# First layer norm of a two-block layer: affine vectors applied at the transposed evacuation, the residual's later by token

## What is computed

```python
def layernorm(x, g, b):
    mu = jnp.mean(xf, axis=-1, keepdims=True)
    xc = xf - mu
    var = jnp.mean(xc * xc, axis=-1, keepdims=True)
    y = xc * lax.rsqrt(var + LN_EPS) * g + b

h = layernorm(x, ln_in_g, ln_in_b)
proj = h @ w_in[l]                       # 2048 x 7184
...
mix = jnp.concatenate([y_conv, y_m], axis=-1) @ w_out[l]
h = layernorm(ALPHA * h + mix, ln1_g[l], ln1_b[l])
```

## Time and profile before

| | us |
|---|---|
| median of three runs | 3107.63 (3106.39 to 3108.59) |
| the profiled execution | 3097.76 |
| its span | 3096.0 |
| TensorE matmul busy | 2666.7 (86%) |
| VectorE busy | 1770.5 (57%) |
| ScalarE busy | 881.6 (28%) |
| mean granted clock of TensorE | 0.985 |

### The profile page before, as it was taken

How to read it: one execution, slowest core, us unless ns; L and a number is a source line. 1 busy time by engine, 2 the same in 40 slices (tenths; PEclk the granted TensorE clock), 3 DMA queues, 4 the chain that set the end, 5 groups by cost and what they waited for, 6 DMA issues and landing times.

```text
span 3096.0 us, 33400 instructions
## 1 busy us (share of the span) xinstructions
PE 2666.7 (86%) x12561; PEld 1914.2 (62%) x12561; DVE 1770.5 (57%) x2212; ACT 881.6 (28%) x943; POOL 532.5 (17%) x532
## 2 busy tenths in 40 slices
PE   6999998677777777777777777999999999999998
PEld 6999888622222222222222237998877888888886
DVE  5456556855555555555555456544656656555445
ACT  3433433300011111111111004433444444444443
POOL 0000000344433343333334430000000000000000
PEclk9999999899999999999999998999999999999999
DMA  6554563899999999999999995544454555555553
GB/s 228 169 172 160 180 228 136 341 422 421 421 422 422 422 422 422 422 422 422 422 422 422 422 356 179 175 156 151 143 190 155 189 190 189 189 189 190 190 193 146
DMA packets 220040, 859.94 MB, mean 278 GB/s; under 512 B 17616, under 2 KB 20016, under 8 KB 147120
## 3 DMA queue, kind: packets, MB, share of 16 engines
q0 software_dynamic: 73728, 536.90, 41.9%
q1 hardware_dynamic: 146224, 321.79, 31.1%
HBM read 856.54 MB, written 2.10 MB: 277 GB/s over the span
## 4 chain that ended last, share of the span: by engine, by line
PE 60%; DMA 30%; DVE 5%; issue 3%; ACT 1%; POOL 0%; POOLq 0%; DVEq 0%; ACTq 0%
DMA vb<-in_peer_v,vidx 29%; PE PS L462 11%; PE PS L2002 7%; PE PS L1860 7%; PE PS L464 5%; PE PS L491 5%; PE PS L495 5%; PE PS L493 5%; PE PS L503 4%; PE PS L507 4%; PE PS L505 4%; DVE wl L396 1%; ACT wh L391 1%; DMA ub<-in_peer_v,vidx 1%; PE PS L1876 1%
## 5 line engine op out<-in xcount | busy, mean ns | idle before, releaser
L1860 PE MATMUL PS<-vb,diag 128*128 128x512 f32 x1920 | 890.0, 607 | 331.4 <-DMA vb<-in_peer_v,vidx 317.3
L396 DVE TENSOR_TENSOR wl<-raw,wh 128x2048 fp32r<-128x2048 f32 x292 | 669.3, 2292 | 732.0 <-ACT wh L391 730.4
L1860 PEld LDWEIGHTS PS<-vb,diag 128*128 128x128 f32 x1920 | 346.3, 190 | 874.4 <-issue 750.6
L1358 DVE CUSTOM_DVE_ANT_0 ub<-ub,RES 128x2048 f32<-128x2048 f32 x256 | 586.5, 2292 | 479.0 <-DMA ub<-in_peer_u,uidx 475.1
L391 ACT CAST wh<-raw 128x2048 fp32r<-128x2048 f32 x292 | 556.7, 1907 | 912.8 <-PE PS L495 292.7
L462 PE MATMUL PS<-XHL,wh 128*128 128x512 f32 x1408 | 488.2, 394 | 0.0
L491 PE MATMUL PS<-XHL,wh 128*128 128x256 f32 x1408 | 402.2, 286 | 7.8 <-DVE XHL L537 4.8
L495 PE MATMUL PS<-XHL,wl 128*128 128x256 f32 x1408 | 399.6, 284 | 0.0
L493 PE MATMUL PS<-XHL,wh 128*128 128x256 f32 x1408 | 399.6, 284 | 0.0
L464 PE MATMUL PS<-XHL,wl 128*128 128x256 f32 x1408 | 390.0, 277 | 0.0
L689 POOL DMA_INDIRECT ub<-in_peer_u,uidx x256 | 261.9, 1023 | 648.2 <-DVE uidx L1346 528.7
(11 more groups left out here) (304 smaller groups left out, 2166.6 us busy)
## 6 DMA issues: line engine op xcount, KB each, us to landing
raw<-in_w_in SPq DMA_DIRECT2D x112, 1024.0 KB, 5.1
raw<-in_w_ffn_gate SPq DMA_DIRECT2D x44, 1024.0 KB, 5.2
raw<-in_w_ffn_up SPq DMA_DIRECT2D x44, 1024.0 KB, 5.1
raw<-in_w_ffn_down SPq DMA_DIRECT2D x44, 1024.0 KB, 4.8
raw<-in_w_out SPq DMA_DIRECT2D x32, 1024.0 KB, 5.1
raw<-in_peer_wq SPq DMA_DIRECT2D x16, 1024.0 KB, 5.1
ub<-in_peer_u,uidx POOLq DMA_INDIRECT x256, 16.5
vb<-in_peer_v,vidx POOLq DMA_INDIRECT x240, 15.3
```

Source lines behind the costliest of these rows:

```text
L396: dve.tensor_tensor(wl[u % 2][:], raw[u][:], wh[u % 2][:].bitcast(F32), ALU.subtract).then_inc(lo_full[u % 2], 1)
L1358: dve.tensor_tensor_reduce(ub[k % RING][:], ub[k % RING][:], RES[:, tb, :], 1.0, 0.0, ALU.mult, ALU.add, dots[:, tb, k:k + 1]).then_inc(S. ...
L1860: m = pe.matmul(PS[:, 4 * tb + b, :], diag[:, k, :], vb[k % RING][:, b * W:(b + 1) * W], start=start and k == 0, stop=False, skip_group_ch ...
```

## The change

The norm of x is split in two. Tokens are only centred and scaled, by token: block 0 on ScalarE in four quarters (`centre_x`, `rstd * x - mean * rstd`, the latter in `nshift`), block 1 on VectorE in four quarters (`xhat`). TensorE turns each quarter as it comes, into PSUM laid out with both blocks of a chunk side by side (`x_wide`). The affine vectors now lie along the partitions: two loads of 8 KB bring them as 32 rows of 128 (`GB`), one transpose and one copy make `gbc`, [128, 2 x 16]. ScalarE applies them while it reads PSUM, 256 columns at a time into a new tile `XA`, from which it casts the high part and VectorE takes the low part, unit by unit; TensorE's unit 0 of slab 0 needs only chunks 0 to 3. ScalarE splits weight unit 0 ahead of x unit 0, and weight unit 1 ahead of x units 1 to 3. `GAIN` and `BIAS` are loaded behind the weights, and `RES` is multiplied by the one and added to the other on VectorE during slab 3, one pass over a block per unit. `tm_ready` counts from two less everywhere.

```diff
@@ layout
+    nshift = at("nshift", SM + 0.9375, [1])
+    gbc = at("gbc", SM + 0.96875, [2 * DC])
+    GB = at("GB", PH + 8.25, [P])
+    XA = at("XA", PH + 9, [2, 4, T])
@@ SyncE
         load_x(0)
+        sp.dma_start(GB[0:DC, :], inp["ln_in_g"].rearrange("(c p) -> c p", p=P)).then_inc(S.gb_in, 16)
+        sp.dma_start(GB[DC:2 * DC, :], inp["ln_in_b"].rearrange("(c p) -> c p", p=P)).then_inc(S.gb_in, 16)
         load_x(1)
-        sp.dma_start(GAIN[:], row(inp["ln_in_g"], D)).then_inc(S.gain_in, 16)
-        sp.dma_start(BIAS[:], row(inp["ln_in_b"], D)).then_inc(S.norm_in, 16)
         w_in = w_view(inp["w_in"])
         for u in range(UNITS):
             load_first(u)
+        sp.dma_start(GAIN[:], row(inp["ln_in_g"], D)).then_inc(S.gain_in, 16)
+        sp.dma_start(BIAS[:], row(inp["ln_in_b"], D)).then_inc(S.norm_in, 16)
@@ ScalarE
+        def centre_x():
+
+            act.wait_ge(S.shift_ready, 1)
+            for q in range(4):
+                y = slice(q * W, q * W + W)
+                act.activation(RES[:, 0, y], RES[:, 0, y], ACT.Identity, bias=nshift[:],
+                               scale=rstd[:, 0:1]).then_inc(S.xhat, 1)
+
+        def first_hi(u):
+
+            act.wait_ge(S.xt_ps, 5 + u)
+            if u >= 2:
+                act.wait_ge(S.xt_lo, 2 * u - 2)
+            for c in range(UC):
+                d = u * UC + c
+                act.activation(XA[:, u % 2, c, :], x_wide(d), ACT.Identity, bias=gbc[:, DC + d:DC + d + 1],
+                               scale=gbc[:, d:d + 1]).then_inc(S.xa_ready, 1)
+            act.wait_ge(S.xa_ready, UC * u + UC)
+            act.copy(XH[:, u * UC:u * UC + UC, :], XA[:, u % 2, :, :]).then_inc(S.xt_hi, 2)
+
         root(0, rstd[:, 0:1])
+        centre_x()
         root(1, rstd[:, 1:2])
-        x_hi(act, 0, 0, 4)
-        lead(act, split_hi, S_IN)
-        x_hi(act, 0, 4, 8)
+        split_hi(act, S_IN, 0)
+        act.wait_ge(S.gb_cols, 1)
+        first_hi(0)
+        split_hi(act, S_IN, 1)
+        for u in range(1, UNITS):
+            first_hi(u)
@@ VectorE
             inverse_root(tb, rstd[:, tb:tb + 1], mv[:, tb, 1:2], LN_EPS)
-        dve.wait_ge(S.gain_in, 16)
-        for tb in range(TB):
-            link(dve.scalar_tensor_tensor(RES[:, tb, :], RES[:, tb, :], mv[:, tb, 0:1], GAIN[:],
-                                          ALU.subtract, ALU.mult))
+            if tb == 0:
+                dve.scalar_tensor_tensor(nshift[:], mv[:, 0, 0:1], -1.0, rstd[:, 0:1], ALU.mult,
+                                         ALU.mult).then_inc(S.shift_ready, 1)
+                dve.wait_ge(S.gb_ps, 1)
+                dve.tensor_copy(gbc[:], PS[:, 7, 0:2 * DC]).then_inc(S.gb_cols, 1)
+                dve.wait_ge(S.gb_cols, 1)
+        for q in range(4):
+            y = slice(q * W, q * W + W)
+            dve.tensor_scalar(RES[:, 1, y], RES[:, 1, y], mv[:, 1, 0:1], rstd[:, 1:2], ALU.subtract,
+                              ALU.mult).then_inc(S.xhat, 1)
+
+        def first_lo(u):
+
+            dve.wait_ge(S.xt_hi, 2 * u + 2)
+            dve.tensor_tensor(XL[:, u * UC:u * UC + UC, :], XA[:, u % 2, :, :], XH[:, u * UC:u * UC + UC, :].bitcast(F32),
+                              ALU.subtract).then_inc(S.xt_lo, 2)
+
+        def residual_gain(tb):
+
+            dve.wait_ge(S.gain_in, 16)
+            link(dve.tensor_tensor(RES[:, tb, :], RES[:, tb, :], GAIN[:], ALU.mult))
+
+        def residual_bias(tb):
+
             dve.wait_ge(S.norm_in, 16)
-            link(dve.scalar_tensor_tensor(RES[:, tb, :], RES[:, tb, :], rstd[:, tb:tb + 1], BIAS[:],
-                                          ALU.mult, ALU.add), S.tm_ready)
+            link(dve.tensor_tensor(RES[:, tb, :], RES[:, tb, :], BIAS[:], ALU.add))
+
         split_lo(dve, S_IN, 0)
-        x_lead(0, S_IN)
+        first_lo(0)
+        split_lo(dve, S_IN, 1)
+        for u in range(1, UNITS):
+            first_lo(u)
@@ VectorE's events of slabs 0 to 13
+            [(3, 2 * tb, lambda tb=tb: residual_gain(tb)) for tb in range(TB)],
+            [(3, 2 * tb + 1, lambda tb=tb: residual_bias(tb)) for tb in range(TB)],
@@ TensorE
+    def x_wide(d):
+
+        return PS[:, d // 2, (d % 2) * T:(d % 2) * T + T]
         pe.wait_ge(S.ident_ready, 1)
-        turn_x(pe, 0, RES)
+        pe.wait_ge(S.gb_in, 32)
+        pe.transpose(PS[:, 7, 0:2 * DC], GB[0:2 * DC, :], ident[0:2 * DC, 0:2 * DC]).then_inc(S.gb_ps, 1)
+        pe.wait_ge(S.gb_cols, 1)
+        for tb in range(TB):
+            for q in range(4):
+                pe.wait_ge(S.xhat, 4 * tb + q + 1)
+                for d in range(4 * q, 4 * q + 4):
+                    m = pe.transpose(x_wide(d)[:, tb * P:tb * P + P], RES[:, tb, d * P:d * P + P], ident[:])
+                m.then_inc(S.xt_ps, 1)
@@
-            pe_slab(pe, s // 2, s % 2, s not in (4, 5, 12, 13), m_events, s, (S.xt_lo, 5) if s == 0 else None)
+            pe_slab(pe, s // 2, s % 2, s not in (4, 5, 12, 13), m_events, s, (S.xt_lo, 2, 2) if s == 0 else None)
```

More of the change, by code:

```diff
@@ L113, in build @@
         gain_in = sem("gain_in")
+        gb_in = sem("gb_in")
+        gb_ps = sem("gb_ps")
+        gb_cols = sem("gb_cols")
+        shift_ready = sem("shift_ready")
+        xhat = sem("xhat")
+        xa_ready = sem("xa_ready")
         norm_in = sem("norm_in")
@@ L475, in pe_slab @@
             if x_in:
-                pe.wait_ge(x_in[0], x_in[1] + u)
+                pe.wait_ge(x_in[0], x_in[1] + u * x_in[2])
             mm_unit(pe, u, buf, cm).then_inc(w_free[u % 2], 1)
@@ L518, in turn_x @@
         for tb in tbs:
-            pe.wait_ge(S.tm_ready, 2 * n + tb + 1)
+            pe.wait_ge(S.tm_ready, 2 * n + tb - 1)
             for q in range(4):
@@ L655, in _ @@
                 load_unit(sp, i + S_DOWN, u, wdn[ds(i * UNITS + u, 1)].rearrange("o p b n -> (o p) b n"))
-        sp.wait_ge(S.tm_ready, 8)
+        sp.wait_ge(S.tm_ready, 6)
         sp.dma_start(GAIN[:], row(inp["final_norm_gain_2"], D)).then_inc(S.norm_in, 16)
@@ L846, in soft @@
             act.activation(eexp[:], tops[:], ACT.Exp, bias=nmx[:, 0:1], accum_out=esum[:]).then_inc(S.soft_exp, 1)
-        act.wait_ge(S.tm_ready, 4)
+        act.wait_ge(S.tm_ready, 2)
         run_slabs(act, split_hi, S_WQ, 4, plan(
@@ L1501, in _ @@
         x_lo(dve, 2, 4, 5)
-        dve.wait_ge(S.tm_ready, 6)
+        dve.wait_ge(S.tm_ready, 4)
         split_lo(dve, S_IN2, 1)
@@ L1825, in _ @@
         for s in range(S_IN, S_OUT):
-            pe_slab(pe, s // 2, s % 2, s not in (4, 5, 12, 13), m_events, s, (S.xt_lo, 5) if s == 0 else None)
+            pe_slab(pe, s // 2, s % 2, s not in (4, 5, 12, 13), m_events, s, (S.xt_lo, 2, 2) if s == 0 else None)
         out_events = plan([(0, 0, lambda: m_turn(1)), (3, 2, turn_keys)])
         for s in range(S_OUT, S_OUT + 4):
-            pe_slab(pe, s // 2, s % 2, False, out_events, s - S_OUT, (S.mix_lo, 1) if s == S_OUT else None)
+            pe_slab(pe, s // 2, s % 2, False, out_events, s - S_OUT, (S.mix_lo, 1, 1) if s == S_OUT else None)
         pe.wait_ge(S.keyT, 4)
@@ L1848, in _ @@
         for s in range(S_WQ, S_WQ + 4):
-            pe_slab(pe, s // 2, s % 2, True, wq_events, s - S_WQ, (S.xt_lo, 13) if s == S_WQ else None)
+            pe_slab(pe, s // 2, s % 2, True, wq_events, s - S_WQ, (S.xt_lo, 13, 1) if s == S_WQ else None)
         scores(3)
@@ L1974, in _ @@
             pe_slab(pe, s // 2, s % 2, n not in (4, 5, 10, 11, 12, 13), in2_events, n,
-                    (S.xt_lo, 21) if n == 0 else None)
+                    (S.xt_lo, 21, 1) if n == 0 else None)
         for s in range(S_OUT2, S_OUT2 + 4):
             pe_slab(pe, s // 2, s % 2, False, plan([(0, 0, lambda: g_turn(1))]), s - S_OUT2,
-                    (S.mix_lo, 5) if s == S_OUT2 else None)
+                    (S.mix_lo, 5, 1) if s == S_OUT2 else None)
         pe.wait_ge(S.mix_y, 4)
```

## The result

| | before | after |
|---|---|---|
| median of eight, the two kernels side by side | 3107.02 (3105.61 to 3108.59) | 3123.85 (3113.33 to 3128.88, and one of 3834.08) |
| ratio, after to before | | 1.0049, 95% interval 1.0034 to 1.0063 |
| the profiled execution | 3097.76 | 3123.98 |
| its span | 3096.0 | 3122.2 |
| first product of slab 0 | 29.13 | 19.43 |

A forecast was written before the change was run, and what follows sets the result against it. TensorE's chain of waits was taken to bound the kernel (TensorE 60%, indirect gathers 30%), with a serial start. A start gain of 11.5 us, kept to the end, took the median from 3107.63 to 3096.1; 8-in-10 range 3092.5 to 3101.5.

The forecast's parts named there:

- Rival F: Expert layer: gathers run another way when started 11 us earlier; 2% of their 317.3 us wait, 6.3, either way; chance 0.05.
- the prediction's last sentence: Gathers: if the first product comes early but the time does not fall, the difference of the waits for `vb` holds the gain.
- the 9.9 that the prediction left open: Whole kernel: gap between profiled execution and median of timed runs, placed outside a start of 30 us and taken as unchanged.
- E: Start: small `GB` loads are overtaken by the big ones, first product at 36.2, 7.1 later than now; 3114.7; chance 0.03.
- First product at 19.0: Start, slab 0: the rebuilt road gives TensorE's first product at 19.0 against 29.13, 10.1 us earlier.
- The rule 0.30 for 128 columns plus 0.845 ns for each further one: ScalarE at the start: estimated activation cost, giving 0.62 for 512 columns (at most 0.7 alone) and 0.41 for 256.
- C: Start: something ahead of the first unit is late, table loads (gain 7.4) or weights not brought forward (7.1); 3100.4; chance 0.12.
- A: First slab: the forecast itself, TensorE at the high clock from the first product, gain 11.5; chance 0.48.
- B: First slab: low clock, by a fall in the pause or by the page's rule, gain 10.1; 3097.5; chance 0.27.
- End of the slab 43.6: First slab at 2.4 GHz from the first product, with a stall to 32.1: end at 43.6, gain 11.6.
- a cover of 1.18 us: Slab 3: VectorE idles 3.47 us ahead of each split, a residual pass takes 2.29, so the passes cost nothing.
- D: Slab 3: the residual passes aren't hidden; at full price 9.2 is lost, gain 2.3; 3105.3; chance 0.05.

The follow-up runs named there:

- the version with forty idle instructions: Changed kernel plus forty idle VectorE instructions ahead of the expert loop, five per unit in slabs 4 and 5: 3098.39, ratio 0.9981 to the kernel before.
- the one with five: Kernel before plus five idle VectorE instructions ahead of the expert loop, nothing else: 3132.71, ratio 1.0078.
- the version with nine idle instructions: Changed kernel plus nine idle VectorE instructions ahead of the expert loop, fourteen with its own five: 3097.04, ratio 0.9969 to the kernel before.
- twelve: Kernel before plus 12 idle VectorE instructions ahead of the expert loop: 3122.39, one profiled execution.
- the two versions that priced the start: Changed kernel plus forty idle instructions, with GAIN and BIAS loaded ahead of the weights again (3094.34), or with the four residual passes replaced by idle instructions (3091.46).
- the first four experiments: Five idle VectorE instructions ahead of the expert loop (3132.71), five behind it (3105.94), 261 ahead (3132.38), each on the kernel before; forty ahead on the changed kernel (3098.39).

## Why the prediction was wrong

**What failed.** The change was costed as work: durations, waits, queues, and what hides them. Its length in instructions was not a term of the sum. The step that says "The change touches only what stands ahead of the first product and, later, VectorE's spare time" is the one that failed: what the change does to everything behind it on VectorE, which it moves by five places of the program, was put at nothing without a reason. It measured 27.4 us. From what I had then, two things spoke for asking: the loop was over 256 instructions long, and that page of the Trainium skill says that a branch out of two blocks is paid for. How near to the edge the kernel stood (one instruction) could have been read from its compiled program, to one place or so, once one length that stalls was known. Its price, 4.6 to 5.5 us for each return here (23.2 to 27.5 in five), could not: no row of the kernel before shows such a stall.

**Rival F** named the place, the gathers, and the prediction's last sentence the sign to look for, the difference of the waits for `vb`. In the totals it seems to fail, 317.3 before and 317.8 after:

```profile
PE PS L1933 <- DMA vb<-in_peer_v,vidx: 317.8, 233, 2.7
PE PS L1933 <- ACT diag L903: 28.5, 2, 27.2
```

But a wait is booked to whatever ended last, and the first one of the layer, 26.9 us before and 27.2 after, is booked to `vb` before and to `diag` after. Without it TensorE waits 290.4 us for `vb` before and 317.8 after, while its other waits for `diag` fall from 14.1 to 1.3: 14.6 more in all. So the sign was there, under a change of names. The page's group of these products shows the whole loss, half in idle time and half in longer products (count | busy us, mean ns | idle before), before and after:

```profile
L1860 PE MATMUL PS<-vb,diag 128*128 128x512 f32 x1920 | 890.0, 607 | 331.4 <-DMA vb<-in_peer_v,vidx 317.3
```

```profile
L1933 PE MATMUL PS<-vb,diag 128*128 128x512 f32 x1920 | 902.2, 614 | 346.2 <-DMA vb<-in_peer_v,vidx 317.8
```

12.2 and 14.8 us, 27.0 together; the first part goes with a granted clock that falls behind a stall (0.89 from 844 to 860). F's size, 2% of 317.3 or 6.3 us, was too small by four times. And its mechanism is refuted: the gathers begin at 601.12 in the version with forty idle instructions and keep their pace, and begin at the old time in the one with five and lose it. A chance of 0.05 for it, 0.05 for slower in all, was an underestimate of what a change to one engine's program can do elsewhere.

**Where the time went**, in the profiled executions: 26.2 = 27.4 in the expert layer + 9.4 in the MLP - 10.6 at the start. The first is shown, by ten runs. The second isn't the change's: the version with nine idle instructions runs the MLP at 44.37, and the kernel before with thirteen, whose source has nothing else new, at 45.23. It would also explain the 9.9 that the prediction left open between the profiled 3097.76 and the median 3107.63: 11 trips of 0.86 are 9.4, if the profile had the quicker pace and the three timed runs, which have no trace, the other.

**The start, step by step.** The two small loads landed 4.6 and 4.4 us after their issue, ahead of x block 1: `GB` was turned at 6.31 and copied at 9.36, wanted at 9.4. E is out.
- First product at 19.0, came at 19.43. The parts that were bounded by nearest rows are those that missed: four centring quarters 2.93 us against 4 x 0.62 to 0.7; four activations of 256 columns 1.93 against 4 x 0.41 = 1.64. The rule 0.30 for 128 columns plus 0.845 ns for each further one comes out some 15% low; an activation with two vectors per partition costs 0.48 and 0.73.
- Transposes from 10.44 (10.1) and the first weights split at 12.68 (12.8), with no wait for their load: the load had landed. VectorE's quarters took 1.92 us, 13.01 to 14.93, instead of the 2.47 taken. Block 1's first was turned at about 14.9, where 14.3 to 14.6 was forecast.
- No table load for Identity, so that part of C is out; the other part of C is what the old order of loads does, 23.11 against 22.0 forecast for it, with the weights ready at 16.78 against 15.9.
- The granted clock in the first slab: 1.00 in the changed kernel (A), 0.50 in the version with nine (B), and both in the version with forty. The windows (start:end, length, busy us of PE, PEld, DVE, ACT, POOL, PEclk, DMA share, GB/s) of the changed kernel:

```profile
16.00:19.00 3.00, 0.10 (x1) 0.00 (x0) 2.06 (x2) 2.91 (x4) 0.00 (x0) 1.00 1.07 393
19.00:20.00 1.00, 0.57 (x5) 0.60 (x6) 0.49 (x2) 1.00 (x2) 0.00 (x0) 1.00 1.11 444
20.00:25.00 5.00, 5.00 (x44) 5.00 (x43) 3.31 (x2) 4.83 (x10) 0.00 (x0) 1.00 1.02 393
```

  A and B differ by less than the forecast's 1.5 us. The slab ends at 44.71 with the first and 45.51 with the second, and under A the wait for `wl` takes back 1.67. That wait was forecast as 1.6, and ScalarE free for weights 2 at 27.9 (came 28.56). Which of the two clocks is met lay, as said, on the edge: the first product at 19.43 found 1.00 after a pause of 3.33 us, at 19.57 found 0.50 after 3.12, and in the version with forty, after 3.33 again, the products run fast from 19.08 and slow from 20.57 (0.28 us each, then 0.42).
- The rule that transposes don't bring the full clock (the Trainium skill, TensorE: Matmul & The Clock Gate, Part 4) has the changed kernel against it: only transposes stand ahead of its first product, and that product and all of the 5 us from 20.00 run at 1.00 (0.28 us a product, where it is 0.41 at 0.50). The clock column alone is no proof so early: it reads 1.00 from 0 us on in both kernels, also over the first sixteen transposes of the kernel before, which take 3.65 us where the second sixteen take 1.97. The pace tells them apart, as the prediction read it; the column doesn't.
- End of the slab 43.6, came 44.71; gain kept 11.5, came 10.5 there and 10.6 at the expert layer. So the sum was 0.9 us too kind; ScalarE's activations carry 0.7 of it (free at 28.56 against 27.9).
- Slips in the working, on which nothing rests: 19.5 and three units of 2.85 are 28.05, not 27.9; three table loads of 1.28 would put the first product at 22.8, and the 21.7 of C holds two; C's 3100.4 and 1.5 make 3101.9, not 3101.5.
- Residual: a cover of 1.18 us was forecast, and cost nothing. In slab 3 each pass ran, and each next split still had idle time in front of it. VectorE's timeline; it answers to the earlier trace rows:

```profile
107.36 2.28 DVE L1168 TENSOR_TENSOR RES<-RES,GAIN 128x2048 f32<-128x2048 f32 x1
110.99 2.29 DVE L406 TENSOR_TENSOR wl<-raw,wh 128x2048 fp32r<-128x2048 f32 x1 [1.35 <-ACT wh L401]
113.20 2.28 DVE L1173 TENSOR_TENSOR RES<-RES,BIAS 128x2048 f32<-128x2048 f32 x1
116.75 2.29 DVE L406 TENSOR_TENSOR wl<-raw,wh 128x2048 fp32r<-128x2048 f32 x1 [1.26 <-ACT wh L401]
...
127.98 2.29 DVE L406 TENSOR_TENSOR wl<-raw,wh 128x2048 fp32r<-128x2048 f32 x1 [0.97 <-ACT wh L401]
```

  D is out: the cover left is 0.97 to 1.35, and the run without the passes gains nothing.

The working of the start was right to about a microsecond in its sum (its parts missed by up to 0.7), and it decided nothing, since the start was not where the change cost.

## What to carry to other kernels

Count instructions as well as microseconds. VectorE's loop of 269 instructions shows that any edit ahead of such a loop, even one idle instruction, can move it so that it no longer lies in two blocks and each return stalls. The signs are idle rows that end in "issue" once per return at fixed instructions, and more packets on the "instruction" queue than before. Worked out from the two blocks of 256 that the Trainium skill states (the section named above), a loop of L instructions from branch target to branch, with L over 256, fits only at 513 - L of the 256 places. The runs agree for 269, where it is 244; no other length and no other engine was tried. Pad with idle instructions ahead of the loop until the rows are gone, and compare two versions of a kernel only when both are clear of it.

And where a total of waits doesn't move although the stage does, look at what the longest wait was booked to.

## What the runs showed of the hardware

**Loading of instructions.** On VectorE, one wait of 5.6 to 7.2 us ahead of the loop's first work and one of 1.5 to 2.8 us at the boundary, or one of 10.4 to 10.8 where these fall together; the pair raises the time of a gather-bound trip (two steps of 79.5 us) by about 5. The stalls add up to 7.8 to 8.9 us a return (10.4 to 10.8 with twelve) and cost less. The likely reason, not tested, is that part of each falls into time in which VectorE would have waited for a gather anyway: 2.14 us at that place in the kernel before.

**Two paces of the MLP.** In the second block's MLP the products run at one of two paces, and with them all 11 trips. The group of `XHL` by `wh`, 512 columns, on the pages of the changed kernel and of the one with forty idle instructions (count | busy us, mean ns | idle before):

```profile
L472 PE MATMUL PS<-XHL,wh 128*128 128x512 f32 x1408 | 497.6, 399 | 0.0
```

```profile
L472 PE MATMUL PS<-XHL,wh 128*128 128x512 f32 x1408 | 488.2, 394 | 0.0
```

The same two values, 497.6 and 488.2, stand on the pages of the kernel before with thirteen idle instructions and with fourteen. (The mean of one is less sure than the sum: it is 391 beside 488.2 in the two versions that priced the start.) From 2530 to 2574 us TensorE is busy without a pause at a granted clock of 1.00 in the kernel before and in the changed one, and the pace is even within an execution. Each kernel has one trace, so that the pace changes from one execution to the next is read from the times: of nineteen of the kernel before, taken beside the first four experiments, five took 3095.7 to 3099.7 and fourteen 3105.4 to 3108.2. It doesn't go with the stalls of the loop: five idle instructions had stalls and 45.23 us a trip, twelve had stalls and 44.37, thirteen no stalls and 45.23. What sets it was not found, and it is worth 9.4 us, nearly as much as this change was meant to bring.

**A pause and the clock.** Pauses of TensorE of 3.33 and 3.12 us before the first product were followed by a granted clock of 1.00 and 0.50, the longer one by the higher, and a second pause of 3.33 by 1.00 and, 1.5 us later, by 0.50. The length of the pause alone doesn't say which is met. These are the changed kernel, the one with nine idle instructions and the one with forty.
